# Reordering the border between two blocks of a two-model kernel: output halves by tile, modulation sums, and tile 0's normalisation

## The reference

```python
mod = silu(c) @ w_ada[l] + b_ada[l]
shift, scale, gate = split(mod, 3)
h = rms_norm(x, g_pre[l]) * (1.0 + scale) + shift
proj = h @ w_in[l]          # 1024 -> 3072, then a short convolution, pooling and gates
y = concat([y_a, y_p]) @ w_out[l]      # 1024 -> 1024
x = x + gate * rms_norm(y, g_post[l])
```

## Time and profile before

| | before |
|---|---|
| median of 3 runs | 1284.09 us (1283.38 to 1287.20) |
| time of the profiled execution | 1283.19 us |
| its span, first to last instruction | 1281.5 us |
| mean granted clock of TensorE | 0.993 of 2.4 GHz |
| DVE busy | 887.6 us, 69% of the span |
| ACT busy | 641.2 us, 50% |
| POOL busy | 172.2 us, 13% |

### The profile page before, as it was taken

How to read it: one execution, slowest core, us unless ns; L and a number is a source line. 1 busy time by engine, 2 the same in 40 slices (tenths; PEclk the granted TensorE clock), 3 DMA queues, 4 the chain that set the end, 5 groups by cost and what they waited for, 6 DMA issues and landing times.

```text
span 1281.5 us, 19572 instructions
## 1 busy us (share of the span) xinstructions
PE 1247.1 (97%) x7756; PEld 1110.4 (87%) x7756; DVE 887.6 (69%) x931; ACT 641.2 (50%) x825; POOL 172.2 (13%) x217
## 2 busy tenths in 40 slices
PE   3999999999999999989999999999999999999998
PEld 2899899888888899978988888888889998988887
DVE  6769666676666767987766667666667687766665
ACT  2445545554444456855544444444446676644442
POOL 8400100088200110000100001000001221200000
PEclk9999899999999999999999999999999999999999
DMA  9897495455556362324555554665554444456551
GB/s 364 267 315 270 160 328 179 149 194 184 186 191 196 117 220 66 128 71 131 182 183 194 195 183 147 229 197 187 180 191 160 148 153 151 151 192 196 196 196 66
DMA packets 167104, 236.88 MB, mean 185 GB/s; under 512 B 5172, under 2 KB 146624, under 8 KB 164992
## 3 DMA queue, kind: packets, MB, share of 16 engines
q1 hardware_dynamic: 165920, 234.57, 54.8%
q0 software_dynamic: 816, 0.89, 0.3%
q10 hardware_dynamic: 304, 0.53, 0.1%
HBM read 234.92 MB, written 1.05 MB: 184 GB/s over the span
## 4 chain that ended last, share of the span: by engine, by line
PE 86%; DVE 6%; DMA 4%; ACT 2%; POOL 1%; issue 1%; DVEq 0%; ACTq 0%; POOLq 0%
PE acc L2191 23%; PE acc L2193 12%; PE acc L2227 5%; PE acc L2228 5%; PE acc L2229 5%; PE acc L2209 4%; PE acc L2210 3%; PE acc L2211 3%; DVE wlo L1355 2%; DMA raw<-in_w_in_dram 2%; PE acc L2599 2%; PE acc L2245 2%; PE acc L2128 2%; DVE region L1362 1%; PE acc L2129 1%; PE acc L2130 1%
## 5 line engine op out<-in xcount | busy, mean ns | idle before, releaser
L1355 DVE TENSOR_TENSOR wlo<-raw,whi 128x2048 fp32r<-128x2048 f32 (+1 forms) x199 | 453.8, 2283 | 200.1 <-ACT whi L746 199.2
L746 ACT ACTIVATE whi<-raw 128x2048 fp32r<-128x2048 f32 (+1 forms) x199 | 378.1, 1904 | 183.5 <-PE acc L2229 113.1
L2191 PE MATMUL acc<-hT,whi 128*128 128x512 f32 x1280 | 320.2, 392 | 0.5 <-ACTq L827 0.5
L2191 PEld LDWEIGHTS acc<-hT,whi 128*128 128x128 f32 x1280 | 232.4, 189 | 43.9 <-issue 0.7
L2193 PEld LDWEIGHTS acc<-hT,wlo 128*128 128x128 f32 x1280 | 174.6, 190 | 12.5
L2193 PE MATMUL acc<-hT,wlo 128*128 128x256 f32 x1280 | 178.5, 282 | 0.0
L2227 PE MATMUL acc<-whi,sT_hi 128*128 128x512 f32 x320 | 125.0, 391 | 0.0
L2228 PE MATMUL acc<-wlo,sT_hi 128*128 128x512 f32 x320 | 125.0, 390 | 0.0
L2229 PE MATMUL acc<-whi,sT_lo 128*128 128x512 f32 x320 | 124.5, 389 | 0.0
L2209 PE MATMUL acc<-whi,hT 128*128 128x256 f32 x416 | 120.2, 289 | 1.1 <-DVE hT L1429 1.1
L2210 PE MATMUL acc<-wlo,hT 128*128 128x256 f32 x416 | 117.6, 283 | 0.0
(11 more groups left out here) (324 smaller groups left out, 1952.2 us busy)
## 6 DMA issues: line engine op xcount, KB each, us to landing
raw<-in_ffn_w_in_dram SPq DMA_DIRECT2D x88, 1024.0 KB, 5.1
raw<-in_ffn_w_out_dram SPq DMA_DIRECT2D x44, 1024.0 KB, 5.0
raw<-in_w_ada_dram SPq DMA_DIRECT2D x24, 1024.0 KB, 5.6
raw<-in_w_in_dram SPq DMA_DIRECT2D x24, 1024.0 KB, 6.0
raw<-in_diff_w_in_dram SPq DMA_DIRECT2D x12, 1024.0 KB, 5.2
raw<-in_nsa_w_in_dram SPq DMA_DIRECT2D x10, 1024.0 KB, 5.3
raw<-in_w_out_dram SPq DMA_DIRECT2D x8, 1024.0 KB, 5.0
raw<-in_nsa_cmp_w_dram SPq DMA_DIRECT2D x4, 1024.0 KB, 5.5
```

What stands on the lines that cost most here:

```text
L746: nc.scalar.activation(whi[:, w % SPL, 0:n], raw[:, r % RAW, 0:n], ACT.Copy).then_inc(hi_ready, 1)
L1355: nc.vector.tensor_tensor(wlo[:, w % SPL, 0:n], raw[:, r % RAW, 0:n], whi_f[:, w % SPL, 0:n], ALU.subtract).then_inc(raw_done, 1)
L2191: nc.tensor.matmul(o, hi[:, kt, cs], hT[:, :, kt, :], start=kt == 0, stop=False)
```

## The change

Four edits, all at the border of block 0 and block 1.

1. Block 0's last two output chunks also run with `tile_first=True`.
2. The modulation sums for block 1 move from behind the output product into `out_pair`, right behind tile 0's last part and ahead of tile 1's four remaining parts.
3. DVE normalises tile 0 at the end of tile 0's turn in the loop, ahead of tile 1's gate product; before, it stood inside tile 1's turn.
4. DVE's three small modulation operations move with it, and now stand ahead of the normalisation instead of behind it.

```diff
@@ DVE, the loop over the tiles at the end of block 0
                     step(nc.vector.tensor_tensor(
                         xn[:, tt, :], acc[:, 4 + 2 * tt:6 + 2 * tt, :].rearrange("p b n -> p (b n)"),
                         gate_row[:, :], ALU.mult))
-                    if tt:
-                        normalise(0, 4)
-                        modulation(1, 0)
                     dve.wait_ge(rs_ready, n_rs)
                     nc.vector.scalar_tensor_tensor(out=x[:, tt, :], in0=xn[:, tt, :], scalar=rs[:, 2 + tt:3 + tt],
                                                    in1=x[:, tt, :], op0=ALU.mult, op1=ALU.add).then_inc(x_ready, 1)
                     if tt == 0:
                         stream_to(w_at[("in1", 1, IN1_ORDER[0])])
+                        modulation(1, 0)
+                        normalise(0, 4)
@@ PE
-            def out_pair(w_a, kts_a, ready_a, w_b, kts_b, ready_b, entry=None, tile_first=False):
+            def out_pair(w_a, kts_a, ready_a, w_b, kts_b, ready_b, entry=None, tile_first=False, modulate=False):
...
                 for tt, nh in early:
                     part(w_b, kts_b, tt, nh).then_inc(y_ps, 1)
+                if modulate:
+                    sum_modulation(1, 0)
                 if tile_first:
                     part(w_a, kts_a, 1, 0)
                     part(w_b, kts_b, 1, 0).then_inc(y_ps, 1)
...
-                         entry=0 if l else None, tile_first=bool(l))
+                         entry=0 if l else None, tile_first=True, modulate=l == 0)
                 n_s += 4
-                if l == 0:
-                    sum_modulation(1, 0)
```

## The result

The changed kernel takes 1289.12 us (median of 15 runs, 1285.22 to 1292.22), the kernel before 1283.96 us (15 runs beside it, 1281.15 to 1288.34). The ratio is 1.0035 with a 95% interval of 1.0022 to 1.0048: 4.5 us slower, 2.8 to 6.2. The forecast was 1288.3 us, 0.33% above the 1284.09 us of before that it started from.

A forecast was written before the change was run, and what follows sets the result against it. TensorE, busy for 97% of the span, was taken as the bound. ACT's order (2.55 us) plus the clock (1.7) gave 4.25 us, so 1288.3 us against the median 1284.09; range 1284.4 to 1291.6.

The forecast's parts named there:

- Tile 0's halves first: Ahead of output chunk b: tile 0 complete no sooner, gap grows by 1.36 us; gain nothing, cost on PE 1.36 us.
- The sums inside: Ahead of tile 1's last 24 products: modulation row's wait hidden, sums take 3.40 us, tile 1 ends at 144.99 us.
- DVE's order: Tile 0's normalisation starts 0.8 us early but buys nothing, because PE reaches the transposes only at 144.83 us.
- ACT's order: Behind tile 1's product, ACT's square and high half precede tile 0's features, so PE restarts 2.55 us later.
- The clock: At the sums: falls to 1.2 GHz and slows tile 1's 24 products behind them; 1.7 us taken, bounds from nothing.
- The second low stretch: At block 1's restart: low clock costs some 1.7 us in both kernels and stays, as PE idles longer ahead of it.
- The sum: Whole border: 2.55 + 1.7 = 4.25 us slower, 1288.3 us against the median; chance 0.45.
- 2: Rival: clock at 2.4 GHz when block 1 restarts, saving 1.7 us, and no fall in the sums; 1284.9 us, chance 0.09.
- 3: Rival: tile 0's normalisation sets the restart, ACT's work for tile 1 not being ahead; 1282.7 us, chance 0.04.
- 1: Rival: ACT's order costs 2.55 us, but the clock holds through the sums; 1286.6 us, chance 0.24.
- 4: Rival: gap and sums trip the clock early, or it stays low longer; 3.4 to 5 us, 1290 to 1291.6, chance 0.18.

The follow-up runs named there:

- e9: e4 plus two idle products on PE ahead of its wait for chunk b; median 1286.46 us, ratio to before 1.0010.
- e8: Changed kernel with tile_first=False in block 0 and the sums in three groups (four, four, eight); median 1284.97 us, ratio to before 0.9990.
- e1: Kernel before with tile_first=True in block 0 and nothing else; median 1285.21 us, ratio to before 1.0001.
- e4: Changed kernel with the sixteen sums spread in four groups of four between the output parts; median 1286.78 us, ratio to before 1.0025.
- e6: Changed kernel with five idle products behind tile 0's transposes, in PE's wait ahead of the restart; median 1288.62 us, ratio to before 1.0008.
- e2: Changed kernel with tile_first=False again in block 0, the sums still unbroken; median 1286.65 us, ratio to before 1.0020.
- e11_turn_earlier: e5_best with tile 1's transposes behind 32 products of tile 0 instead of 48; median 1285.67 us, ratio to before 1.0000.
- e5_best: Changed kernel with tile_first off, sums in three groups, ACT's and DVE's lists reordered, tile 0's 48 products ahead of tile 1's transposes; median 1285.91 us, ratio 0.9997.

## Why the prediction was right

**Tile 0's halves first: right.** Tile 0 was not complete sooner behind b, and the gap grew by 1.32 us (1.36 forecast). The price of the part, 1.36 us, measured 1.49 by two runs with the clock up (e9 less e8). What the step left to a rival, and what three of the runs with this part showed (e1, e4, e6), is that a longer gap can also lower the clock.

**The sums inside: right.** PE took them up 2.86 us behind b without a wait for the last modulation row. They took 3.49 us (3.40 forecast).

**DVE's order: right, and worth nothing.** Normalisation began 9.83 us behind b instead of 10.61, 0.78 us earlier (0.8 forecast); PE came 2.9 us after it was done.

**ACT's order: the mechanism right, not the whole of it.** Tile 1's end to features took 3.15 us (148.81 to 151.96; forecast 3.32 with the hand-over), features to restart 2.81 (2.84). R lay 4.15 us later behind b, against 2.55 + 1.7 = 4.25 forecast. But the prediction said that DVE's gate product and x of tile 1 "fit between". They did, by 0.9 us only: with ACT's high half out of the way they set the restart (18.74 instead of 17.7). The term is the longer of two chains behind tile 1's end, and taking ACT's away gives 0.9 us, not 1.9.

**The clock: right in size, with luck in it, and its place a little off.** It fell at the end of the sums (141.7), not inside them, and 24 products took 148.65 - 141.50 = 7.15 us instead of 5.44: 1.71 us, where 1.7 had been taken from the early low stretch. That this stretch was as long as the early one, 3.4 us, is luck: others at this border lasted 6.8 us (e1, e4) and 10.2 (before). That unbroken sums bring the fall is borne out by all twelve profiles. In the six with unbroken sums the clock fell between 2.8 us into them (before) and 1.5 us behind them (e1, where PE had begun to wait for the halves, so that the wait can be the cause there). In the six with the sums in groups it never fell between the first group and the transposes, and e2, which differs from e8 in nothing but the places of the sums, was 1.5 us longer. The Trainium skill's rule ("TensorE: Matmul & The Clock Gate", Part 1), taken literally, had this term at 0. The traces do not agree: the clock fell in or right behind work that filled PE. The second low stretch, ahead of the restart, stayed as forecast; 4.0 us of it lay behind R, against 4.5 before, which is why 4.15 us at R became 3.91 at C. Its price, 1.7 us in the prediction, is borne out too: R to C took 14.52 us before and 12.78 in e6, with the clock up.

**The sum.** 4.25 us forecast, 3.9 in the profiled border, 4.5 (2.8 to 6.2) in the runs. Of the rivals, 2 and 3 are excluded in the profiled execution. Rivals 1 and 4 may be the same kernel in other executions: the runs spread from 1285.2 to 1292.2 us, and low clock that comes once, twice or not at all would give such a spread. Each run's mean granted clock says that low clock is in it: of the changed kernel's 15 runs the three fastest (up to 1285.4 us) have 0.993, the three slowest (from 1291.6) 0.989 to 0.991. In the first set of before, 32 runs, the five slowest (1289.1 to 1293.4 us) have 0.983 to 0.987, all others 0.991 to 0.995. Where in the program the clock was low is known for the profiled executions alone.

## What to carry to other kernels

Work moved out of an idle stretch of the bottleneck engine and ahead of a product moves everything that waits for that product; read in each other engine's list what stands between that product and the next thing the bottleneck needs, and expect a second list right behind the first. Making one tile ready early pays only if no list has the other tile's work ahead of it. Where a border is short, the clock is a term of the same size as the reordering: break up long runs of tiny products, try filling waits, and check both in the profile, over several executions.

## What was unexpected of the hardware

A gap of 2 to 3 us in PE's work lowered the clock in some executions and not in others. Ahead of chunk b, four gaps came with 3.4 to 6.8 us at 1.2 GHz. With 2.93 and 2.80 us the clock fell inside the gap, 0.8 us before its end; with 3.72 and 2.07 us it fell 1.5 and 1.4 us behind it, while PE was busy. With gaps of 1.91, 1.48, 1.41 and less it did not fall there. Ahead of the restart, the same wait of 3.04 us (two versions that differ behind it only) had the clock fall in one and stand in the other:

```profile
147.90:151.00 3.10, 0.07 (x1) 0.02 (x1) 2.48 (x4) 2.93 (x9) 0.79 (x2) 1.00 0.40 163
```

and the same stretch of the other version:

```profile
147.70:150.70 3.00, 0.00 (x0) 0.00 (x0) 2.45 (x4) 2.87 (x8) 0.79 (x2) 0.82 0.49 201
```

The first is of e11_turn_earlier (PEclk 1.00), the second of e5_best (0.82). A single profile of a kernel with such a gap says little about what its clock costs on average.

POOL's scalar operation L516 took 0.96 or 0.97 us beside DVE's low half and 0.22 or 0.23 otherwise, in both kernels, and it ends when DVE's operation does (144.29 and 144.22). It delays tile 0's inverse root by 0.7 us. Beside DVE's gate product L1637, which reads one of its two inputs from PSUM, it took 0.22 us (at 139.46). The Trainium skill ("SBUF — State Buffer", SBUF: two separate sides) describes an exclusive lock on a port pair that DVE takes for an operation with two inputs in SBUF, and that a GpSimd operation reading SBUF waits for. The trace agrees.
